# The gated-linear-attention output stage in units of one head and half a sequence, where it had units of two heads

## What is computed

```python
o_m = jnp.einsum('bhtk,bhkv->bhtv', q_m[:, :, 0], s_meta)         # chunk 0: 16 meta tokens
o_r = jnp.einsum('bhntk,bhnkv->bhntv', q_r, states)               # 8 chunks of 64 tokens
...
o_gla = rms_norm(o_gla, gla_norm[i].reshape(GLA_HEADS, GLA_DV))   # over the 128 values of a head
o_gla = (o_gla * jax.nn.silu(gr))
```

## Time and profile before

| | |
|---|---|
| median of three runs | 2438.54 us |
| the profiled execution | 2438.54 us |
| its span, first to last instruction | 2437.3 us |
| TensorE busy | 2363.9 us (97%) |
| TensorE's share of the chain that ended last | 91% |
| mean granted TensorE clock | 0.993 |
| GLA output stage of layer 0 / layer 1 | from 128.4 us / from 842.0 us |

### The profile page before, as it was taken

How to read it: one execution, slowest core, us unless ns; L and a number is a source line. 1 busy time by engine, 2 the same in 40 slices (tenths; PEclk the granted TensorE clock), 3 DMA queues, 4 the chain that set the end, 5 groups by cost and what they waited for, 6 DMA issues and landing times.

```text
span 2437.3 us, 36562 instructions
## 1 busy us (share of the span) xinstructions
PE 2363.9 (97%) x15284; PEld 2132.6 (87%) x15284; DVE 1300.8 (53%) x2229; ACT 904.8 (37%) x1526; POOL 96.3 (4%) x111
## 2 busy tenths in 40 slices
PE   7999989999999999999999999999999999999997
PEld 6798989999998798999899879987898877888886
DVE  4345566636643455476446666775744454443443
ACT  4145454314433255454224443322244444221222
POOL 1000010000020000010000020000000001000001
PEclk9999999999999999999999999999999999999999
DMA  3121122322322111133323322222322122232231
GB/s 130 52 75 51 38 91 96 101 74 95 106 63 70 61 62 47 36 112 98 101 79 95 101 69 79 78 87 71 103 70 65 66 87 95 91 114 73 95 118 47
DMA packets 57190, 197.60 MB, mean 81 GB/s; under 512 B 8337, under 2 KB 10803, under 8 KB 57027
## 3 DMA queue, kind: packets, MB, share of 16 engines
q1 hardware_dynamic: 55107, 189.86, 24.0%
q0 software_dynamic: 1344, 4.36, 0.6%
q10 hardware_dynamic: 576, 1.05, 0.1%
HBM read 193.11 MB, written 2.13 MB: 80 GB/s over the span
## 4 chain that ended last, share of the span: by engine, by line
PE 91%; DVE 5%; ACT 2%; issue 1%; DMA 0%; SPq 0%; ACTq 0%; DVEq 0%
PE G L895 73%; PE G L923 7%; PE X L1083 2%; PE X L923 2%; PE X L1063 1%; PE X L1159 1%; PE X L1040 1%; DVE wL L1561 1%; PE X L997 1%; PE X L1117 1%; PE X L1144 1%; DVE aL L1568 1%; PE X L1129 1%; ACT wH L1193 0%; DVE hT L1664 0%
## 5 line engine op out<-in xcount | busy, mean ns | idle before, releaser
L895 PE MATMUL G<-aH,wH 128*128 128x264 f32 (+3 forms) x3248 | 822.6, 317 | 39.5 <-DVE wL L1561 16.4
L895 PE MATMUL G<-aL,wH 128*128 128x264 f32 (+3 forms) x3248 | 795.9, 309 | 0.0
L895 PE MATMUL G<-aH,wL 128*128 128x264 f32 (+3 forms) x3248 | 794.7, 308 | 0.0
L1193 ACT ACTIVATE wH<-raw 128x512 fp32r<-128x512 f32 (+4 forms) x495 | 393.5, 811 | 710.2 <-PE G L895 642.7
L895 PEld LDWEIGHTS G<-aH,wH 128*128 128x128 f32 (+1 forms) x3248 | 529.1, 189 | 76.5 <-issue 27.0
L1561 DVE TENSOR_TENSOR wL<-raw,wH 128x512 fp32r<-128x512 f32 (+4 forms) x495 | 456.7, 933 | 251.7 <-ACT wH L1193 250.5
L895 PEld LDWEIGHTS G<-aH,wL 128*128 128x128 f32 (+1 forms) x3248 | 526.7, 188 | 30.4
L895 PEld LDWEIGHTS G<-aL,wH 128*128 128x128 f32 (+1 forms) x3248 | 527.4, 188 | 27.5 <-issue 0.2
L1664 DVE TENSOR_TENSOR hT<-G,hT 128x528 f32<-128x528 f32 (+1 forms) x88 | 61.4, 698 | 230.9 <-PE G L895 230.9
L895 PE MATMUL G<-hidH,wH 128*128 128x264 f32 (+1 forms) x528 | 140.8, 321 | 1.4 <-DVE hidL L1749 1.4
L895 PE MATMUL G<-hidL,wH 128*128 128x264 f32 (+1 forms) x528 | 141.2, 322 | 0.0
(11 more groups left out here) (276 smaller groups left out, 2749.4 us busy)
## 6 DMA issues: line engine op xcount, KB each, us to landing
raw<-weights SPq DMA_DIRECT2D x272, 512.0 KB, 3.3
raw<-weights SPq DMA_DIRECT2D x48, 704.0 KB, 4.1
raw<-weights SPq DMA_DIRECT2D x16, 384.0 KB, 3.0
negc<-sums POOLq DMA_DIRECT2D x16, 264.0 KB, 3.5
raw<-weights SPq DMA_DIRECT2D x16, 128.0 KB, 2.0
out_t<-hT SPq DMA_DIRECT2D x8, 256.0 KB, 2.1
hT<-x_t ACTq DMA_DIRECT2D x4, 256.0 KB, 5.1
hT<-x_t SPq DMA_DIRECT2D x4, 256.0 KB, 6.7
```

What stands on the lines that cost most here:

```text
L895: done = e.matmul(m.G[g][0:M, bank, 0:n], a[:, k, 0:M], b[:, k0 + k, lo - t0:lo - t0 + n], start=(k == 0 and c == 0), stop=(k == nk - 1 an ...
L1193: e.activation(m.wH[:, i % NW, c], m.raw[:, r, c], ACT.Copy).then_inc(s.w_hi, 1)
```

## The change

A unit u is now one head (u//2) and one half of the tokens (u%2), and there are eight. Unit u uses bank X[u%2] for its output and X[2+u%2] for its sum, and the halves of `gt` and `Sb` with the same number. `go(u)` waits for the multiply of unit u-2 and no longer for that of the last one. In the list, `go(u)` stands one yield ahead of `gn(u-1)`; the stage has 18 yields where it had 20. The waits of other steps are counted anew and mean the same as before.

```diff
-            for v in range(4):
-                step("go", l, v)
+            for u in range(9):
+                if u < 8:
+                    step("go", l, u)
                 yield
-                yield
-                step("gn", l, v)
-                yield
-                yield
+                if u:
+                    step("gn", l, u - 1)
                 yield
...
-    def go(l, v):
-
-        pr, (lo, n) = v // 2, HALVES[v % 2]
-        if v == 0:
+    def go(l, u):
+        h, (lo, n) = u // 2, HALVES[u % 2]
+        pr, q = h // 2, slice(64 * (h % 2), 64 * (h % 2) + 64)
+        if u < 2:
             e.wait_ge(s.state, 9 * l + 9)
         else:
-            e.wait_ge(s.mix_gla, 8 * l + 2 * v)
+            e.wait_ge(s.mix_gla, 8 * l + u - 1)
         for c in range(9):
             t0, nt = (0, 16) if c == 0 else (16 + 64 * (c - 1), 64)
             if lo <= t0 < lo + n:
-                for hh in range(2):
-                    q = slice(64 * hh, 64 * hh + 64)
-                    done = e.matmul(X[:, hh, t0 - lo:t0 - lo + nt], m.S[q, c, pr, :], m.gq[q, pr, t0:t0 + nt],
-                                    start=True, stop=True)
-                    if t0 + nt == lo + n:
-                        done.then_inc(s.go, 1)
-
-    def gn(l, v):
-        n = HALVES[v % 2][1]
-        if v == 0:
+                done = e.matmul(X[:, u % 2, t0 - lo:t0 - lo + nt], m.S[q, c, pr, :], m.gq[q, pr, t0:t0 + nt], start=True,
+                                stop=True)
+        done.then_inc(s.go, 1)
+
+    def gn(l, u):
+        n = HALVES[u % 2][1]
+        if u == 0:
             e.wait_ge(s.gdec_exp, l + 1)
+        elif u == 1:
             e.wait_ge(s.tm_act, 3 * TM_NTH["fv", l])
         else:
-            e.wait_ge(s.gn_ln, 4 * l + v)
-        e.wait_ge(s.go_sq, 4 * l + v + 1)
-        e.matmul(X[:, 2, 0:n], m.ones[:, :], m.gt[:, 0, 0:n], start=True, stop=True)
-        e.matmul(X[:, 3, 0:n], m.ones[:, :], m.gt[:, 1, 0:n], start=True, stop=True).then_inc(s.gn, 1)
+            e.wait_ge(s.gn_ln, 8 * l + u - 1)
+        e.wait_ge(s.go_sq, 8 * l + u + 1)
+        e.matmul(X[:, 2 + u % 2, 0:n], m.ones[:, :], m.gt[:, u % 2, 0:n], start=True, stop=True).then_inc(s.gn, 1)
...
-    def gn(l, v):
-        n = HALVES[v % 2][1]
-        r = m.Sb[:, :, 0:n]
-        if v:
-            e.wait_ge(s.mix_gla, 8 * l + 2 * v)
-        e.wait_ge(s.gn, 4 * l + v + 1)
+    def go(l, u):
+        n = HALVES[u % 2][1]
+        e.wait_ge(s.go, 8 * l + u + 1)
+        if u >= 2:
+            e.wait_ge(s.gn, 8 * l + u - 1)
+        e.activation(m.gt[:, u % 2, 0:n], X[:, u % 2, 0:n], ACT.Square).then_inc(s.go_sq, 1)
...
-        for hh in range(2):
-            h = 2 * (v // 2) + hh
-            e.scalar_tensor_tensor(out=m.mixT[:, h, lo:lo + n], in0=X[:, hh, 0:n], scalar=m.vc(("gla", l), h),
-                                   in1=m.Sb[:, hh, 0:n], op0=ALU.mult, op1=ALU.mult).then_inc(s.mix_gla, 1)
+        e.scalar_tensor_tensor(out=m.mixT[:, h, lo:lo + n], in0=X[:, u % 2, 0:n], scalar=m.vc(("gla", l), h),
+                               in1=m.Sb[:, u % 2, 0:n], op0=ALU.mult, op1=ALU.mult).then_inc(s.mix_gla, 1)
```

More of the change, by code:

```diff
@@ L1034, in ft @@
         if (p, u) == (0, 0):
-            e.wait_ge(s.gn_ln, 4 * l + 4)
+            e.wait_ge(s.gn_ln, 8 * l + 8)
         else:
@@ L1432, in gdec, with gn @@
         e.activation(flat(m.dec[:, :, :]), X[:, 2, 0:16], ACT.Exp, scale=1.0 / 16).then_inc(s.gdec_exp, 1)
-    def go(l, v):
-        n = HALVES[v % 2][1]
-        e.wait_ge(s.go, 8 * l + 2 * v + 2)
-        if v:
-            e.wait_ge(s.gn, 4 * l + v)
-        e.activation(m.gt[:, :, 0:n], X[:, 0:2, 0:n], ACT.Square).then_inc(s.go_sq, 1)
-    def gn(l, v):
-        n = HALVES[v % 2][1]
-        r = m.Sb[:, :, 0:n]
-        if v:
-            e.wait_ge(s.mix_gla, 8 * l + 2 * v)
-        e.wait_ge(s.gn, 4 * l + v + 1)
+    def go(l, u):
[4 more added lines that the diff above has]
+        e.activation(m.gt[:, u % 2, 0:n], X[:, u % 2, 0:n], ACT.Square).then_inc(s.go_sq, 1)
+    def gn(l, u):
+        n = HALVES[u % 2][1]
+        r = m.Sb[:, u % 2, 0:n]
+        if u >= 2:
+            e.wait_ge(s.mix_gla, 8 * l + u - 1)
+        e.wait_ge(s.gn, 8 * l + u + 1)
         lnexp()
-        e.activation(r, X[:, 2:4, 0:n], ACT.Ln, scale=1.0 / 128, bias=m.epsc[:, 0:1]).then_inc(s.gn_ln, 1)
-        e.wait_ge(s.gn_ln, 4 * l + v + 1)
+        e.activation(r, X[:, 2 + u % 2, 0:n], ACT.Ln, scale=1.0 / 128, bias=m.epsc[:, 0:1]).then_inc(s.gn_ln, 1)
+        e.wait_ge(s.gn_ln, 8 * l + u + 1)
         e.activation(r, r, ACT.Exp, scale=-0.5).then_inc(s.gn_exp, 1)
@@ L1727, in rest @@
                 e.wait_ge(s.psum, NTH["evac", i])
-                e.wait_ge(s.mix_gla, 8 * l + 4 * (h // 2) + 3 + h % 2)
+                e.wait_ge(s.mix_gla, 8 * l + 2 * h + 2)
                 e.tensor_tensor(mx, mx, m.gate[:, h % 2, :], ALU.mult).then_inc(*own.one())
@@ L1868, in gst, with gn @@
                     done.then_inc(*own.one())
[L1870 to L1874, removed]
+    def gn(l, u):
+        h, (lo, n) = u // 2, HALVES[u % 2]
+        e.wait_ge(s.gn_exp, 8 * l + u + 1)
+        e.wait_ge(s.go_sq, 8 * l + u + 1)
+        if u == 0:
             e.wait_ge(s.fsum, 3 * l + 3)
-        for hh in range(2):
-            h = 2 * (v // 2) + hh
-            e.scalar_tensor_tensor(out=m.mixT[:, h, lo:lo + n], in0=X[:, hh, 0:n], scalar=m.vc(("gla", l), h),
-                                   in1=m.Sb[:, hh, 0:n], op0=ALU.mult, op1=ALU.mult).then_inc(s.mix_gla, 1)
+        e.scalar_tensor_tensor(out=m.mixT[:, h, lo:lo + n], in0=X[:, u % 2, 0:n], scalar=m.vc(("gla", l), h),
+                               in1=m.Sb[:, u % 2, 0:n], op0=ALU.mult, op1=ALU.mult).then_inc(s.mix_gla, 1)
     def fsum(l):
```

## The result

The changed kernel takes 2453.05 us (median of four runs, 2450.72 to 2453.8). The kernel before takes 2437.75 on the same chip (four runs, 2436.31 to 2438.73). The ratio is 1.0062, with an interval from 1.0049 to 1.0075. So the change costs 15 us.

The account below looks back on a forecast made before the run. TensorE, busy for 97% of the span, was taken as the bound. Per layer 5.4 + 4.4 − 0.3 + 0.4 − 1.3 − 2.2 = 6.4 us, 12.8 for two, on 2438.5 gave 2451; range 2442 to 2460.

Parts of the forecast that it names:

- The `go` passes: GLA output stage: lone passes 0.112 us apart, so eight one-head units each cost what the four old ones did; +5.4 us a layer.
- a lone pass at 0.056: Rival for the GLA output stage: single-head passes 0.056 us apart, −8.1, total 2442 to 2443; 8%, shared with a hidden chain.
- an exposed load (2470): Rival for the GLA output stage: weight loads on the same rows show in every pass, about 0.24 us each, total 2470; 4%.
- The wait in front of `go`: GLA output stage: TensorE waits for the multiply of unit u−2, 1.0 us four times and 0.25 twice; +4.4 us a layer.
- The clock: Start of `part`: full clock instead of 6.83 us at half; −2.2 us a layer, between 0 and −3.1.
- The order: Behind the GLA output stage: FoX steps shift against the foreground; −0.3, +0.4 and −1.3 us a layer.
- The piece at `part`: Start of `part`: `fo(2,6)` replaces `fs(2,8)`, so the wait is about 1.6 us instead of 2.79; −1.3 us a layer.
- The empty slots: Behind the GLA output stage: four foreground slots without a product instead of six; −0.3 us a layer, worth between 0 and 1.6.
- The +0.4 for later `PT` copies: FoX, odd rounds: `fs(s)` and `fo(s−2)` share a slot, leaving the copy one slot of cover, not two; between 0 and 1.5.
- so I expect the clock not to fall: Start of `part`: behind the shorter wait of about 1.6 us the clock stays full, as in FoX's waits of up to 1.2.
- Rival (4): FoX's waits behind its norm, 10.7 us in both layers, shrink with the new places; 2440.5 if all went; 10%.
- Rival (1): Start of `part`: the clock still falls behind the shorter wait; 2455.7 us; 18%.

## Why the prediction was right

The forecast was 2451, and the result 2453.05. Term by term, for one layer:

- **The `go` passes, +5.4.** Measured 5.38, from the stage with the new units and no wait against the old units in the same order. The passes of a unit are on one half of the rows and 0.112 apart. The rivals of a lone pass at 0.056 and of an exposed load (2470) are out, since a unit of ten passes costs 1.46. On the second of these the Trainium skill speaks in "TensorE: Matmul & The Clock Gate": Part 3 has the load overlap only across row groups, while "Step-by-step: what each phase is for" in Part 2 also lets it go ahead into a background buffer. The trace agrees with the latter: loads and passes share their rows in every unit, and the passes are 0.112 apart, no further than pairs were.
- **The wait in front of `go`, +4.4.** Measured 4.11 in layer 0, the changed kernel's stage less the one with `gn` ahead (42.60 − 38.49). Start by start, the waits are 0.19, 0.88, 0.98, 0.20, 0.98 and 0.94: four with one slot of cover and two with two, as the count of slots had it. Each is 0.02 to 0.12 shorter than forecast. In layer 1 they are 0.19, 0.88, 0.98, 0, 0.98 and 0.50, in all 0.6 less: the products that ran at half clock covered that much.
- **The clock, −2.2.** Measured −2.01, where the steps from C to D are the same with half and with full clock (63.41 before, 61.40 in layer 0 of the changed kernel with 20 yields). Like the forecast it is net of what VectorE's work uncovers, here the second wait for `aL`. The mechanism was right and the size near.
- **The order, −0.3 + 0.4 − 1.3 = −1.2.** Measured −2.4: the −4.44 of layer 0 (old units with 18 yields, full clock behind the wait) less the clock's −2.01. So the term was half of what it should have been:
  - The piece at `part` is shorter by 1.40: from the last product pair to `part`'s first it took 3.82 and takes 2.42 (255.76 − 253.34, old units with 18 yields). But in reading it as a gain the prediction erred a little: the piece lost the four passes of `fs(2,8)`, which are only issued earlier, and got those of `fo`. As waiting time, 2.79 to 1.62, it is 1.17.
  - The empty slots are worth nothing (21 yields against 18). The +0.4 for later `PT` copies had the wrong sign: the waits for `PT` went from 2.2 to 1.2 a layer. With the two other lines of FoX's norm, and a new wait of 0.2 for the scaling behind `fo`, TensorE waits 2.1 less a layer, 1.3 ahead of `part` and 0.8 behind it. The prediction had none of this in its sum. The second wait for `aL` is 0.65, where it is 0.93 with 20 yields and full clock.
  - In all, the waits fell by 3.5 a layer, and the order gave 2.4. The other 1.1 shows in the distances between passes. From B to D, the 240 `fo` passes take 25.1 us with 18 yields and 24.3 in layer 0 of the changed kernel with 20, and the last passes of the score steps 2.8 (38 of them) and 2.2 (39). Behind the latter a background pass follows more often than before, where a product pass followed (14 of 27 times ahead of `part`, before 2 of 28), as two background steps now share a slot in every odd round. No run isolates this.

What failed is the step "so I expect the clock not to fall". In layer 0 it fell behind the 1.62 wait, for 3.4 us instead of 6.8, and C to D shows 0.98 more than the same stretch at full clock (61.33 less 60.35, the kernel with `gn` ahead). In layer 1 it didn't fall there. Instead it fell twice among the `go` waits, and the stage took 45.07 where layer 0's took 42.60: 2.47 for two stretches, the 0.6 of covered waits already taken off. This is what the prediction had named as "the clock falls in other places than before". Taken together:

| us for the layer | layer 0 | layer 1 |
|---|---|---|
| lone passes | +5.38 | +5.38 |
| waits in front of `go` | +4.11 | +4.11 |
| the order, and full clock behind the wait | −4.44 | −4.44 |
| the clock fell after all | +0.98 | +2.47 |
| sum | 6.03 | 7.52 |
| from A to D, measured | 6.03 | 7.49 |

So two misses offset each other: the order and full clock gave 1.0 a layer more than the −3.4 forecast for them, and the clock took back 1.0 and 2.5. That the sum came out within 2 us is in part luck; the two largest terms, +5.4 and +4.4, are not. Rival (4), on the side of no loss, came true in part: 4.4 of the 10.7 us of norm waits went. It needed more than 8 to decide. Rival (1), the clock falling at `part` as before, came true in one layer with half the length.

One thing stays open: what decides, with the same steps, whether the clock falls. Behind the same wait of 1.62 it fell in layer 0 of the changed kernel and in layer 1 of the old units with 18 yields, and in both layers with 21; in the other layers of these two, and in both layers of the kernel with `gn` ahead, it didn't. I had no edit that moved only this, and with one trace of each kernel I can't say whether another execution of the same kernel would have it fall in the same places.

The best version is neither kernel: the old units with 18 yields (2430.61) or 21 (2430.72). The gain that lay in the change's order needs one more `yield`. The new units cost far more than it brings: 2 × (5.38 + 4.11) = 19.0 us, before any clock.

## What to carry to other kernels

Before splitting a TensorE step into smaller units, look at which passes run beside each other: two matmuls of 64 contraction rows on different halves cost what one costs (here in fp32, with at most 64 columns), and a unit that keeps only one half pays the full price for half the work. A change that moves steps in an in-order list has two effects, that of the new step and that of the new places; run the list's shift alone, since here it gained 6 us (2430.61 against 2436.9) under a change that lost 15. When a wait is filled with other work, ask first what that work puts ahead of the next operand on the other engines, and which step moves up behind it.

## What the runs showed of the hardware

- Passes on the two row halves overlap almost fully when the halves alternate every two passes (20 passes in 1.06 us, first start to last start, which is the row's 1.33 less one record of 0.27) or every four (1.11), and only at the seam when they alternate every ten (1.78). For the last I had expected no overlap at all.
- A series of short waits was followed by half clock as a long one was. In the changed kernel's layer 1, waits of at most 0.98 (by the starts) among the `go` steps were followed by two stretches of 3.42 at 0.50. In layer 0 the same waits were not, but in layer 0 with 20 yields they were, by one stretch. The stage without these waits had none, in either layer. And a wait of 2.80 was once not followed by one (layer 0 of the changed kernel with 20 yields).
- 6.83 us at half clock behind the wait at `part` cost 2.01, and 3.41 us cost 0.92 and 0.98 there, where VectorE had 2.1 to 2.3 us of work in them. In the GLA output stage, where it had 0.2 to 0.7, a stretch of 3.42 cost 1.24 on average. That the cover makes the difference is my reading; no run isolates it.
- Lone fp32 passes of 64 rows, each with a weight load of its own of 0.19 us on the same rows, started 0.112 us apart, so the loads ran under the passes.
